# Loads of the sliding attention's queries moved from SyncE's DMA queue to ScalarE's, in a hybrid attention block

## What is computed

```python
u = rmsnorm(h, g_pre)
qa, ka, va, za, qf, kf, vf, zf, ff, ga, gf = split(u @ w_in)
y_swa = swa_branch(qa, ka, va, sinks) * silu(za)      # 2 key heads x 4, window of 64-token chunks, meta keys, ALiBi
y_fox = fox_branch(qf, kf, vf, log_sigmoid(ff + b)) * silu(zf)   # 8 heads, causal, forgetting
merged = sigmoid(ga + b0) * (y_swa @ w_up_swa) + sigmoid(gf + b1) * (y_fox @ w_up_fox)
h = h + rmsnorm(merged @ w_out, g_post)
```

## Time and profile before

| | |
|---|---|
| median of 3 runs | 849.58 us (848.36 to 851.98) |
| the profiled execution, its own time | 849.09 us |
| its span in the trace | 847.2 us |
| TensorE busy | 804.2 us (95%) |
| VectorE, POOL, ScalarE busy | 502.9, 350.6, 315.2 us |
| SyncE's queue (q1) | 119.92 MB |
| ScalarE's queue (q10) | 4.26 MB |

### The profile page before, as it was taken

The page is one execution under the profiler, slowest core; times in us unless marked ns, Lnnn a source line. Parts: engine busy times, 40 slices in busy tenths (PEclk is TensorE's granted clock), DMA queues, the critical chain, the costliest instruction groups (busy, mean ns, idle before and its releaser), DMA issues.

```text
span 847.2 us, 12887 instructions
## 1 busy us (share of the span) xinstructions
PE 804.2 (95%) x4514; PEld 649.7 (77%) x4514; DVE 502.9 (59%) x1050; ACT 315.2 (37%) x645; POOL 350.6 (41%) x292
## 2 busy tenths in 40 slices
PE   3999989999999999999999989799998999999996
PEld 3999989988878878788788855566665688878885
DVE  7944788256776777645646347485878844442222
ACT  6432241333333333333333236365676323222111
POOL 4412214354435435444344325556785444412221
PEclk9999999999999999999999999799999999999999
DMA  9341425369857346365364598996900375443221
GB/s 291 103 125 52 127 64 133 91 168 265 242 163 204 111 139 196 95 173 169 95 182 111 140 231 216 240 245 140 243 3 2 109 238 149 125 163 111 95 79 74
DMA packets 121795, 124.99 MB, mean 148 GB/s; under 512 B 29970, under 2 KB 91874, under 8 KB 121732
## 3 DMA queue, kind: packets, MB, share of 16 engines
q1 hardware_dynamic: 120292, 119.92, 52.3%
q10 hardware_dynamic: 1440, 4.26, 1.3%
HBM read 90.93 MB, written 34.92 MB: 149 GB/s over the span
## 4 chain that ended last, share of the span: by engine, by line
PE 81%; DVE 9%; DMA 3%; issue 3%; ACT 2%; SPq 1%; POOL 1%; DVEq 0%; ACTq 0%; POOLq 0%
PE PS L1837 18%; PE PS L1838 18%; PE PS L1839 18%; PE PS L2084 3%; PE PS L2086 3%; PE PS L2085 3%; PE PS L2007 3%; PE PS L1944 2%; DVE t_val L1589 2%; DMA VF<-v_dram 2%; PE PS L1987 2%; PE PS L1988 1%; PE PS L2022 1%; PE PS L2037 1%; DVE t_lo L1597 1%
## 5 line engine op out<-in xcount | busy, mean ns | idle before, releaser
L1140 POOL TENSOR_TENSOR ops<-s_sum,ops 128x512 fp32r<-128x512 f32 x64 | 87.4, 1376 | 114.3 <-ACT ops L1238 114.3
L1837 PE MATMUL PS<-t_hi,ops 128*128 128x512 f32 x256 | 101.1, 395 | 0.0
L1838 PE MATMUL PS<-t_lo,ops 128*128 128x512 f32 x256 | 99.8, 390 | 0.0
L1839 PE MATMUL PS<-t_hi,ops 128*128 128x512 f32 x256 | 99.8, 390 | 0.0
L1140 POOL TENSOR_TENSOR ops<-raw,ops 128x512 fp32r<-128x512 f32 x48 | 65.0, 1355 | 69.8 <-ACT ops L1238 69.7
L1209 POOL TENSOR_TENSOR acc<-acc,p_fox 128x400 f32<-128x400 f32 (+5 forms) x76 | 62.2, 839 | 5.9 <-ACT p_fox L1362 3.6
L1161 POOL TENSOR_TENSOR w_plain<-raw,w_plain 128x1024 fp32r<-128x1024 f32 x10 | 28.0, 2804 | 85.3 <-ACT w_plain L1267 85.3
L1668 DVE TENSOR_TENSOR z_tmp<-u,PS 128x512 f32<-128x512 f32 x48 | 33.0, 687 | 48.9 <-PE PS L1839 28.2
L1362 ACT ACTIVATE p_fox<-PS,neg_c_col 128x512 f32<-128x512 f32 (+5 forms) x112 | 54.1, 534 | 21.1 <-PE PS L1993 15.8
L1238 ACT ACTIVATE ops<-s_sum 128x512 fp32r<-128x512 f32 x64 | 39.6, 624 | 54.9 <-DVE s_sum L1470 41.1
L1839 PEld LDWEIGHTS PS<-t_hi,ops 128*128 128x128 f32 x256 | 48.1, 188 | 10.6
(11 more groups left out here) (203 smaller groups left out, 2198.9 us busy)
## 6 DMA issues: line engine op xcount, KB each, us to landing
raw<-in_w_in_dram SPq DMA_DIRECT2D x34, 512.0 KB, 5.2
q_dram<-stage_b SPq DMA_DIRECT2D x32, 256.0 KB, 3.1
g_dram<-stage_b SPq DMA_DIRECT2D x32, 256.0 KB, 2.0
tanh_g<-g_dram SPq DMA_DIRECT2D x16, 512.0 KB, 4.2
max_k<-k_dram SPq DMA_DIRECT2D x16, 260.0 KB, 5.3
max_c<-neg_c_dram SPq DMA_DIRECT2D x8, 520.0 KB, 6.5
x_all<-in_x_dram SPq DMA_DIRECT2D x8, 512.0 KB, 7.7
raw<-in_w_in_dram SPq DMA_DIRECT2D x16, 256.0 KB, 4.6
```

What stands on the lines that cost most here:

```text
L1140: nc.gpsimd.tensor_tensor(ops[:, i % OPS, 1], op_source(p, name), ops[:, i % OPS, 0].bitcast(F32), ALU.subtract).then_inc(op_ready, 1)
L1837: pe.matmul(dst, hi_w, hi, start=first, stop=False)
L1838: pe.matmul(dst, hi_w, lo, start=False, stop=False)
L1839: return pe.matmul(dst, lo_w, hi, start=False, stop=last)
```

## The change

The function that loads half a pair's sliding queries takes the queue as an argument. For pair 0 SyncE still calls it, at the same two places. For pairs 1 to 3, six calls in all, ScalarE calls it, after the exps of the tile and before the exps of the item just scored, after the same wait for `ms_filled`. Tiles, shapes, semaphores and all counts stay. In the changed kernel the three requests are L853 to L855 for either engine; some other lines shift by 3 or 7.

```diff
+        def load_queries_swa(queue, j, half):
+            cols = slice(half * BANK, (half + 1) * BANK)
+            q_hi, q_lo = (qd[j, x].rearrange("(g r) t -> r g t", g=2)[:, :, cols] for x in range(2))
+            queue.dma_start(QAs[Q0, :, cols].bitcast(F32), q_hi).then_inc(q_swa_loaded[half], 16)
+            queue.dma_start(QAs[Q1, :, cols].bitcast(F32), q_hi).then_inc(q_swa_loaded[half], 16)
+            queue.dma_start(QBs[Q0, :, cols].bitcast(F32), q_lo).then_inc(q_swa_loaded[half], 16)
...
@@ SyncE's program @@
-            def load_queries(j, half):
...
@@ the loads of pair 0, twice @@
-                        load_queries(0, 0)
+                        load_queries_swa(sp, 0, 0)
...
-                load_queries(0, 1)
+                load_queries_swa(sp, 0, 1)
...
@@ SyncE, loop over the attention steps @@
-                    elif kind == "score" and st["t"] % 4 == 3 and st["j"] + 1 < PAIRS:
-                        sp.wait_ge(ms_filled, st["ms"] + 1)
-                        load_queries(st["j"] + 1, st["t"] // 4)
...
@@ ScalarE, loop over the attention steps, between "tile" and "exp" @@
+                elif kind == "score" and st["t"] % 4 == 3 and st["j"] + 1 < PAIRS:
+                    act.wait_ge(ms_filled, st["ms"] + 1)
+                    load_queries_swa(act, st["j"] + 1, st["t"] // 4)
```

## The result

Before: 849.32 us (median of 18 runs, 846.79 to 851.98). After: 851.62 us (18 runs, 850.29 to 857.8). The ratio is **1.0034**, interval 1.0021 to 1.0048: slower by some 2 to 4 us, inside the 0.5% called no change. The forecast was 852.8, slower by 0.4%. The total came near; the profile shows that it came out of the wrong term.

The account below looks back on a forecast made before the run. TensorE, busy for 95% of 847.2 us, was taken as the bound. To the profiled 849.09 us were added 3.1 for VF, 0.6 for ScalarE and 0 for SyncE: 852.8 us, range 847.3 to 856.5.

Parts of the forecast that it names:

- The second half of pair 1 changes its place: Start of pair 1: on ScalarE's queue, query loads move before VF's last bytes, so TensorE waits 3.1 us longer.
- do they share?: Question whether DMA engines alternate between both queues; taken as yes from loads at kernel start, giving 3.1 us, otherwise 0.
- rival 1: Only issue time moves: VF lands as now, leaving ScalarE's 0.6 us; 849.7 us, chance 0.24.
- In about 8 us or less: Sign of being right: pair 1's second half of the queries lands in about 8 us or less.
- SyncE is freed: SyncE saves about 1.93 us per group, but full DMA engines mean VF lands no earlier; taken as 0.
- Rival 2: Faster: SyncE's full queue has room sooner, so the stall for VF shrinks; 847.8 or 844.0 us, chance 0.12.
- ScalarE issues 18 DMAs: Six groups at 1.93 us each on ScalarE leave 1.2 us of later exps; half counted, 0.6 us slower.
- TensorE runs about one tile ahead, so I count half: Step that counted 0.6 us of the 1.2 us of later ScalarE exps, between 0 and 1.2.
- Added wait: ScalarE's wait for ms_filled before each group costs 0, as the following exp needs a maximum from the same score.
- Rival 3: Slower: ScalarE's request is held at a full queue, as SyncE's 9.60 us one; about 860 us, chance 0.14 with milder forms.
- If the span changes in a stage other than attention: Sign that the whole account is wrong: the time changes outside the attention stage.
- VF lands at 540.7 or earlier: Sign of being wrong, pointing to the two rivals without a later VF; the forecast had VF landing near 543.8.

Follow-up runs that it names:

- half0: Changed kernel, but only the three first-half groups (after items 3, 11, 19) on ScalarE, the others back on SyncE; 852.88 us, ratio 1.0034 to the kernel before.
- half1: Changed kernel, but only the three second-half groups (after items 7, 15, 23) on ScalarE, the others back on SyncE; 850.32 us, ratio 1.0004 to the kernel before.
- skip11: Changed kernel with the group after item 11 back on SyncE, the other five on ScalarE; 850.09 us, ratio 1.0000 to the kernel before.
- only11: Only the group after item 11 asked for by ScalarE, the other five on SyncE; 852.43 us, ratio 1.0032 to the kernel before.
- issue_only: Kernel before, all queries on SyncE, plus three 4 KB copies to spare DRAM asked for by ScalarE at the six places; 852.56 us, ratio 1.0040.
- again: The changed kernel as it is, run once more beside later runs; 852.5 us, ratio 1.0023 to the kernel before.
- nudge: Changed kernel with one tiny POOL memset ahead of POOL's add of unit 22; 850.09 us, ratio 1.0000 to the kernel before.

## Why the prediction was right, and where not

- *"The second half of pair 1 changes its place", 3.1 us: wrong.* The step that failed is "If the engines share their time between the queues, three transfers can be put before VF's last bytes". They do share once both queues move, but the queries' first bytes move too late. The DMA view of the changed kernel by queue (packets, MB, share), for 516 to 522, 522 to 530 and 536 to 540:

```profile
q1 hardware_dynamic: 491, 1.52, 105.5%
```

```profile
q1 hardware_dynamic: 352, 1.24, 65.9%
q10 hardware_dynamic: 344, 0.64, 36.5%
```

```profile
q1 hardware_dynamic: 1158, 1.32, 111.1%
q10 hardware_dynamic: 12, 0.02, 1.6%
```

  ScalarE asks at 516.50 and the first packet of its queue moves at 522.20, 5.7 us later. It asks at 535.38 and the first packet moves at 539.83, 4.5 us later; until 540 there are 12 packets. VF had landed at 539.44, so not one packet of these queries stood in its way. From the start of movement on, the two queues go side by side (36.5% and 65.9%), so "do they share?" had the right answer for the wrong question: the earlier trace rows tell what happens with queues that both already move, and the question was how long a newly asked transfer takes to move at all behind a backlog. I had that as the second half of rival 1 ("the queries' first bytes come too late"), at 0.24, and for this term it is what happened; rival 1's time, 849.7, is not. "In about 8 us or less" was about met by the landings, 7.7 to 8.7 us after the requests, and means nothing by itself: VF was already there.
- *"SyncE is freed", 0: right as far as the time goes.* In this profile VF was asked for 1.93 us earlier and landed 1.25 us earlier. Over all profiles, the first tile of pair 1 comes this long after the first request for `y`: 28.9 us in the six with both early groups on ScalarE (27.7 to 29.9), 29.9 in the six with neither (29.1 to 30.4), 31.6 in half0 with the first group alone, and 29.7 in half1 with the second alone. That is a gain of 1 us with overlapping spreads, not seen where only the group ahead of VF was moved (one profile), and in time nothing (skip11, which has both: 1.0000). Rival 2's premise, that SyncE's long request gives way sooner, fails in its length (9.84 us against 9.60); it only began 1.93 us earlier.
- *"ScalarE issues 18 DMAs", 0.6 us: right in mechanism, mis-sized.* Each group costs 1.9 us, as counted; the leftover at item 11 is 0.87 us where 0.70 was worked out, and at item 19 0.58 where it was 0.42. The step that failed is "TensorE runs about one tile ahead, so I count half". At item 11 it is not a share of 0.7 us, it is 2.7 us (only11, 1.4 to 3.9), where an order between VectorE and POOL turns; at the other five places it is nothing that can be measured in the time. In the trace, the group at item 19 puts the next score 0.34 us later, and 0.2 us of that is left at item 24.
- *Added wait, 0: not tested.* Nothing speaks against it, and no run tried it by itself.
- *Rival 3, ScalarE held at a request: no.* Its requests take 0.58 to 0.79 us, in the middle of the backlog too.
- *"If the span changes in a stage other than attention":* the changed kernel's profile loses another 1 us from the up projection to the end, 0.9 of it in a wait in the out stage (TensorE for `wo_lo_late`). issue_only, again and nudge have that wait too, with 0.7, 0.5 and 0.4 us, and the other ten have not. Four slow kernels of eight show it, so the sign is met in part and its cause is open; only11, which has the whole loss, does without it.

The sum was 852.8, 851.62 was measured. That is luck: 3.1 us that did not happen stood in for 2 us more at item 11. By its own list of signs, VF's wait (3.1 us, not 6.8) and landing (539.4, not 543.8) were wrong, and "VF lands at 540.7 or earlier" stood among the signs of being wrong. The second half's landing and ScalarE's request of about 0.6 us were right. Of the later exps, item 19 (0.58 us) lies within 0.4 to 0.7 and item 11 (0.87) above it.

## What to carry to other kernels

Asking for loads on a compute engine's queue is paid in that engine's program: three requests were 1.9 us of ScalarE. What such a delay costs does not follow from its length. Groups that made the exps 1.2 and 0.6 us late (items 3 and 19) cost nothing that could be measured in the time, the one that made them 0.9 us late (item 11) cost the whole 0.3%, and the same group put into a gap of 2.7 us cost nothing. Before counting on a second queue to overtake a first one, look how long it takes to move its first packet behind a backlog, not only whether both share the engines. And where adds of VectorE and GpSimd on SBUF start within 0.05 us of each other in the trace, take their order as undecided and price both orders, with the clock that TensorE may lose by the longer wait.

## What was not expected of the hardware

- In the changed kernel, ScalarE's queue moved its first packet 5.7, 4.5, 5.9, 1.6, 4.3 and 1.4 us after the first request of the six groups (items 3, 7, 11, 15, 19, 23), against 1.3 us at the start of the kernel. SyncE's transfers kept the DMA engines busy (104% to 119%) during all of these delays but the last (13%), the 1.6 us included, so busy engines alone do not make the long ones; no run varied it. The Trainium skill (DMA: Bandwidth & Descriptors, Queues, rings and completion order) has the engines go round the queues a packet at a time; the trace agrees once both move (36.5% and 65.9% of the engines' time in 522 to 530). The delay before that is not explained by it.
- The order of two adds that start 0.01 to 0.05 us apart decides which of them takes 1.1 us (VectorE, 0.69 to 1.79) or 0.5 us (POOL, 1.28 to 1.80) more, and with it 0.87 us of TensorE's time. In all eight profiles where VectorE was second, a stretch at the lower granted clock followed and cost some 1.5 us more.
- With one tiny memset added, the twelve runs of a kernel fall into two groups with medians of 848.4 and 853.3 us (nudge), and nothing between 850.6 and 852.6. A median of such a kernel says little; its list of runs has to be read.
